# Weight copies of the next projection behind heads 1 and 2, and six recurrence tiles split during the last keys' projection

## What is computed

```python
h = rms_norm(x, attn_norm[l])
z = h @ w_in[l]
q_lat, kv_lat, k_rope_raw, g_mla, u_lru, g_lru, m_mla, m_lru = jnp.split(z, IN_SPLITS, axis=-1)
y_mla = mla_branch(q_lat, kv_lat, k_rope_raw, g_mla, cos, sin, ...)
y_lru = rglru_branch(u_lru, g_lru, conv_w[l], conv_b[l], ...)   # (h * silu(gate)) @ w_o_lru
merged = jax.nn.sigmoid(m_mla) * y_mla + jax.nn.sigmoid(m_lru) * y_lru
x = x + merged @ w_out[l]
ple_gate = jax.nn.sigmoid(rms_norm(x, ple_norm[l]) @ w_ple_gate[l])
x = x + (p[l] @ w_ple[l]) * ple_gate
```

```python
q = (rms_norm(q_lat, q_a_norm) @ w_q_b)      # per head 128 plain and 64 rotary columns
kv = (rms_norm(kv_lat, kv_a_norm) @ w_kv_b)  # per head 128 key and 128 value columns
s = (q_nope . k_nope + q_rope . k_rope) * scale
pr = softmax(where(mask, s, -inf)); o = pr @ v
return (o * silu(gate)) @ w_o
```

## Time and profile before

| | |
|---|---|
| runs (us) | 2049.51, 2050.53, 2049.27; median 2049.51 |
| profiled execution | 2050.18 us, span 2048.4 us, mean granted TensorE clock 0.991 |
| TensorE busy | 1998.9 us, 98% of the span |
| VectorE busy | 677.3 us, 33% |
| ScalarE busy | 715.6 us, 35% |
| GpSimd busy | 898.1 us, 44% |
| DMA | 247.20 MB, mean 121 GB/s |

### The profile page before, as it was taken

The page is one execution under the profiler, slowest core; times in us unless marked ns, Lnnn a source line. Parts: engine busy times, 40 slices in busy tenths (PEclk is TensorE's granted clock), DMA queues, the critical chain, the costliest instruction groups (busy, mean ns, idle before and its releaser), DMA issues.

```text
span 2048.4 us, 24912 instructions
## 1 busy us (share of the span) xinstructions
PE 1998.9 (98%) x9070; PEld 1663.5 (81%) x9070; DVE 677.3 (33%) x943; ACT 715.6 (35%) x1240; POOL 898.1 (44%) x683
## 2 busy tenths in 40 slices
PE   7999999999999999999999999899999999999996
PEld 6888888888888888888888877778888888888885
DVE  4100000000454638354555544681010250111344
ACT  6322223222253444433344544322222222333333
POOL 3444444444454545454451223154444454444552
PEclk9999999999999999999999999999999999999998
DMA  6433333333233323332462332254333343234232
GB/s 253 170 123 108 117 123 119 128 123 124 82 99 107 114 91 107 104 134 82 114 161 66 124 103 81 84 205 144 104 122 123 112 185 113 83 103 186 102 103 103
DMA packets 128697, 247.20 MB, mean 121 GB/s; under 512 B 15053, under 2 KB 40309, under 8 KB 120565
## 3 DMA queue, kind: packets, MB, share of 16 engines
q1 hardware_dynamic: 116688, 185.09, 27.9%
q10 hardware_dynamic: 11941, 61.17, 7.9%
HBM read 214.26 MB, written 29.36 MB: 119 GB/s over the span
## 4 chain that ended last, share of the span: by engine, by line
issue 60%; POOL 38%; POOLq 1%; DVE 1%; PE 0%; ACT 0%; DVEq 0%
POOL wlo L362 38%; POOLq L361 1%; POOLq L358 0%; DVE x L1270 0%; PE ps L1281 0%; DVE x L1243 0%; DVE stage L1242 0%; DVE x L1273 0%; POOLq L362 0%; ACT stage L811 0%; DVEq L126 0%; DVE nrm L848 0%; DVE nrm L853 0%; DVE nrm L854 0%; DVE nrm L847 0%
## 5 line engine op out<-in xcount | busy, mean ns | idle before, releaser
L362 POOL TENSOR_TENSOR wlo<-raw,whi 128x512 fp32r<-128x512 f32 x672 | 896.8, 1338 | 1124.7 <-ACT whi L378 1123.7
L378 ACT ACTIVATE whi<-raw 128x512 fp32r<-128x512 f32 x672 | 421.8, 631 | 1159.6 <-PE ps L1281 1109.7
L1281 PE MATMUL ps<-hhi,whi 128*128 128x512 f32 x1408 | 548.2, 389 | 1.1 <-POOL wlo L362 1.1
L1281 PE MATMUL ps<-hhi,wlo 128*128 128x512 f32 x1408 | 547.8, 389 | 0.0
L1281 PE MATMUL ps<-hlo,whi 128*128 128x512 f32 x1408 | 547.7, 389 | 0.0
L1281 PEld LDWEIGHTS ps<-hhi,whi 128*128 128x128 f32 x1408 | 264.3, 188 | 56.5 <-POOL wlo L362 1.5
L1281 PEld LDWEIGHTS ps<-hlo,whi 128*128 128x128 f32 x1408 | 264.4, 188 | 55.1 <-issue 0.2
L1281 PEld LDWEIGHTS ps<-hhi,wlo 128*128 128x128 f32 x1408 | 264.4, 188 | 54.7
L933 DVE TENSOR_TENSOR stage<-ps,stage 128x512 f32<-128x512 f32 x16 | 11.0, 691 | 412.4 <-ACT stage L475 410.9
L1281 PE MATMUL ps<-lhi,whi 128*128 128x512 f32 x256 | 101.2, 395 | 6.0 <-POOL wlo L362 3.8
L1281 PE MATMUL ps<-llo,whi 128*128 128x512 f32 x256 | 100.8, 394 | 0.0
(11 more groups left out here) (254 smaller groups left out, 2438.8 us busy)
## 6 DMA issues: line engine op xcount, KB each, us to landing
raw<-in_w_in SPq DMA_DIRECT2D x88, 1024.0 KB, 5.0
raw<-in_w_o_lru SPq DMA_DIRECT2D x16, 1024.0 KB, 5.0
raw<-in_w_o_mla SPq DMA_DIRECT2D x16, 1024.0 KB, 5.0
raw<-in_w_out SPq DMA_DIRECT2D x16, 1024.0 KB, 5.0
raw<-in_w_ple_gate SPq DMA_DIRECT2D x16, 1024.0 KB, 4.9
sig_scr<-stage ACTq DMA_DIRECT2D x8, 1024.0 KB, 7.0
raw<-in_w_kv_b SPq DMA_DIRECT2D x32, 256.0 KB, 3.9
stage<-sig_scr ACTq DMA_DIRECT2D x8, 1024.0 KB, 4.8
```

The costliest lines, as they stand in the source:

```text
L362: pool.tensor_tensor(wlo[:, k % RING], raw[:, k // RAWC, k % RAWC], whi[:, k % RING].bitcast(F32), ALU.subtract).then_inc(lo_ready, 1)
L378: act.activation(whi[:, c % RING], raw[:, c // RAWC % 2, c % RAWC], ACT.Copy).then_inc(hi_ready, 1)
L1281: return pe.matmul(o, l, r, start=start, stop=stop)
```

## The change

ScalarE's four copies of the next projection's weights stood one behind head 1's exponentials, one behind head 2's and two behind head 3's. Now two stand behind head 1's and two behind head 2's. The loop variable `h` in this code is one ahead of the head whose `turned_hi` runs, and the exponentials in it are those of head `h`.

VectorE's `split_merge` of tiles 0 to 3 is taken out of the last group's heads. Tiles 0 to 5 (`AHEAD = 6`) are split at the head of the last group, ahead of the keys' `projection_lo`, so while TensorE projects that group's keys. Behind the group the tiles 6 to 15 remain.

```diff
                         exp(h, 2)
                         exp(h, 1)
                         exp(h, 0)
-                        split(c + 2 * KL + RING + h - 1)
+                    if h < 3:
+                        split(c + 2 * KL + RING + 2 * h - 2)
+                        split(c + 2 * KL + RING + 2 * h - 1)
                     if h == 3:
-                        split(c + 2 * KL + RING + 3)
                         act.wait_ge(exp_done, 16 * g + 16)
                         act.sem_inc(released[ks], 1)
...
+            AHEAD = 6
+
...
             for g in range(NG):
                 pt = 1 - g % 2
 
+                if g == NG - 1:
+                    dve.wait_ge(l_landed, 16)
+                    for t in range(AHEAD):
+                        split_merge(lhi, llo, l_split, t)
                 projection_lo(g, 1, range(4))
...
-                if g == NG - 1:
-                    dve.wait_ge(l_landed, 16)
                 for h in range(1, 5):
...
-                    if h < 3 and g == NG - 1:
-                        split_merge(lhi, llo, l_split, 2 * h - 2)
-                        split_merge(lhi, llo, l_split, 2 * h - 1)
...
-            for t in range(KL, KD):
+            for t in range(AHEAD, KD):
```

## The result

The changed kernel takes 2017.56 us (2017.3 to 2018.58, four runs) where the kernel before takes 2049.82 (2049.27 to 2050.53, four runs): a ratio of 0.9843, interval 0.9826 to 0.986, or 32.3 us less. The prediction was 2016.2 in a range of 2013.5 to 2022.0. The profiled execution took 2017.5 us with a span of 2015.7, against 2050.18 and 2048.4.

The account below looks back on a forecast made before the run. TensorE, busy 98% of the span, bounds the kernel through its idle and half-rate time. Savings of 25.8 + 4.25 + 3.9 - 0.6 = 33.3 us gave a span of 2016.9 and a median of 2016.2 us, range 2013.5 to 2022.

Parts of the forecast that it names:

- The stops and their half rate: TensorE before each next projection's third weight chunk: four stops for `wlo` and half-rate matmuls behind them vanish, saving 25.8 us.
- Rival (a): TensorE behind the stops: only idle goes, something else keeps the half rate; 2030.2 us, chance 0.08.
- Rival (c): GpSimd's third `wlo` stays late, by ring slot or raw row; only the tile parts gain, 2042.0 us, chance 0.04.
- ScalarE's cover: Before ScalarE's next exponential: 0.51 us more copying fits in 0.85 us of idle, leaving 0.34; cost nothing.
- Rival (d): ScalarE's copies delay exponentials in eight places, TensorE waits and falls to half rate; 2056.9 us, chance 0.03.
- VectorE's `pjlo`: Attention heads: if GpSimd's extra tile held it, it would end 0.8 us later, inside 1.65 us of cover.
- The tiles out of the heads: Last group's heads 1 and 2: without VectorE's split tiles, TensorE needs group three's time, saving 4.25 us.
- the stop for `llo`: Recurrence output's fifth chunk: 2.18 us stop and 1.71 us of half rate behind it vanish, saving 3.9 us.
- Tile 7: Recurrence output, next to be late: ready 2.2 us on, while TensorE wants it 5.4 us on.
- The wait for `qr`: Last group's first scores: six tiles meeting GpSimd's make `knlo` 2.2 us late, so TensorE waits about 0.6 us.
- several subtractions of 1.7 us: Sign of a wrong forecast: VectorE's six moved tiles showing several subtractions this long.
- The bound behind it: Upper bound for the `qr` wait: 1.1 us if four block, plus at most 2.9 us of half rate, 4.0.

Follow-up runs that it names:

- e6: Changed kernel with all four of ScalarE's copies behind head 1's exponentials, instead of two there and two behind head 2's: 2019.68 us.
- e1: Changed kernel with VectorE's tiles taken back into the heads, so only ScalarE's copies are moved: 2025.3 us, ratio 0.9885 to the kernel before.
- the repeat: Later comparison of the same changed kernel, nothing altered, with the kernel before: 2016.98 us against 2048.21, ratio 0.9846.
- e3: Changed kernel with four tiles split at the head of the last group in place of six: 2021.59 us.
- e2: Changed kernel with ScalarE's copies back in their old places, so only VectorE's six tiles are moved: 2041.78 us, ratio 0.9962 to the kernel before.

## Why the prediction was right

**The stops and their half rate (25.8 us): right.** With the copies alone, the first three group distances shrink by 18.86 us, from 196.70 to 177.84 (first scores at 1088.65 and 1266.49), where 6.76 + 6.23 + 5.91 = 18.90 were predicted. The way from the stop to the transposes is 3.22 us at clock 1.00. Rival (a), that something else holds the clock down, is out: the half rate went with the stops. Rival (c) is out by GpSimd's rows.

**ScalarE's cover (nothing): right, and thin.** 0.31 us of idle is left, and `e6` lost 0.4 us per group with the exponential 0.61 us late. Rival (d) needed 2.5 us per place; 0.61 us late is more than the 0.51 that it feared of a copy, and it halved no clock. VectorE's `pjlo`, which the prediction had only bounded, was not held by GpSimd's extra tile: in the changed kernel it ran beside GpSimd's pair of 1110.22 to 1112.80 and took 1.78 us, where the earlier trace rows has 1.77.

```profile
1112.07 1.78 DVE L1124 TENSOR_TENSOR pjlo<-ps,pjhi 128x256 fp32r<-128x256 f32 x3 [0.60 <-ACT pjhi L699]
```

**The tiles out of the heads (4.25) and the stop for `llo` (3.9): right.** The second row of the ledger is 13.35 against 13.31, the third 1.65 against 1.71. Tile 7, the next in line, was not late.

**The wait for `qr` (-0.6): right in kind, 0.2 too large.** VectorE in the last group, from the first tile to `knlo` (the six tiles' casts and subtractions, then the projection's low tiles), with two of GpSimd's rows of the same time:

```profile
1250.79 0.43 DVE L1092 CAST lhi<-llo 128x512 fp32r<-128x512 f32 x1
1251.25 1.66 DVE L843 TENSOR_TENSOR llo<-llo,lhi 128x512 fp32r<-128x512 f32 x1
...
1253.28 0.69 DVE L843 TENSOR_TENSOR llo<-llo,lhi 128x512 fp32r<-128x512 f32 x1
1253.89 1.51 DVE L1092 CAST lhi<-llo 128x512 fp32r<-128x512 f32 x1
...
1256.51 1.66 DVE L843 TENSOR_TENSOR llo<-llo,lhi 128x512 fp32r<-128x512 f32 x1
...
1259.15 1.51 DVE L1092 CAST lhi<-llo 128x512 fp32r<-128x512 f32 x1
...
1261.31 2.48 DVE L1083 SCALAR_TENSOR_TENSOR knlo<-ps,knhi 128x512 fp32r<-128x512 f32 x4
...
1250.87 1.49 POOL L362 TENSOR_TENSOR wlo<-raw,whi 128x512 fp32r<-128x512 f32 x1 [3.41 <-ACT whi L378]
...
1253.54 1.59 POOL L362 TENSOR_TENSOR wlo<-raw,whi 128x512 fp32r<-128x512 f32 x1 [1.18 <-ACT whi L378]
```

Four of the twelve instructions meet a GpSimd tile and take 1.66 or 1.51 us, one for each of the four GpSimd tiles, as predicted: two are subtractions, and two are casts, a form that the prediction had not named as one that can be blocked. The six tiles take 10.5 us (1250.79 to 1261.31) instead of 6.4; the prediction's working, 1268.70 to 1279.7, had 11.0. The last group distance is 59.66 against 59.28 with five tiles, 0.4 us. One of the prediction's own signs of being wrong, several subtractions of 1.7 us, did appear, with two of 1.66. It was badly chosen, because the sum had already counted four blocked instructions. The Trainium skill has both forms ("SBUF — State Buffer", section "Who interferes with whom"): a `tensor_tensor` with both inputs in SBUF, and a cast that runs in a mode that takes the shared port pair, shut out a GpSimd instruction that reads SBUF and are shut out by it, and the one that comes second waits for the whole of the other. The rows agree for VectorE, 1.66 against 0.69 and 1.51 against 0.42.

**The bound behind it was mis-sized, to no effect.** The prediction allowed 2.9 us of half rate on top of a wait of 1.1, and argued from stops "of 2 us and more". The chip takes a wait of 2.08 us there without it. In `e1` a wait of 2.17 us for `prob` did bring it, so the length alone doesn't give the bound (the last section comes back to this). The high end of the range, 2022.0, was wider than it needed to be for that reason.

**What is left of the difference.** 2017.56 was measured against 2016.2. By the ledger 0.2 us was gained more than predicted in the stage (33.47 against 33.3), and 0.80 lost in the one profiled execution before the stage, which the repeat does not show. The medians of the changed kernel are 2017.56 and 2016.98, those of the kernel before 2049.51, 2049.82, 2049.7 and 2048.21 in different comparisons. As gains that is 32.3 us and 31.2 in the repeat against 33.3 predicted, and 33.3 lies inside both intervals (28.7 to 35.7 and 28.9 to 34.4 us). The miss of 1.0 to 2.1 us is of the size of the scatter ahead of the stage, and I give it no cause.

## What to carry to other kernels

When a producer that has been idle for microseconds causes a short stop on the bounding engine, look at the place in the order of the instruction that feeds it, before its duration: here the same work done earlier gave 6.4 us per group, of which more than a third was half-rate matmuls behind the stop. Measure the way from the stop to a landmark behind it, not the idle alone, and take the whole of it, since half rate is not a fixed surcharge. Before work is put into an engine's idle time, count how much of it will meet instructions of another engine that hold it up: six tiles took 10.5 us instead of 6.4, and one tile fewer would have been free.

## What the runs showed of the hardware that I had not expected

**Half rate does not follow from the length of a stop alone.** In one place of one program, the first score of group four, 1.15 and 2.08 us left the clock at 1.00, 3.01 us halved it, but 1.2 us after the end of the wait, and 3.93 halved it almost at once. In front of the fifth chunk a stop of 2.18 us was followed by half rate at once in the kernel before, 0.7 us later in `e3`, and not at all in `e1`. What TensorE did just before doesn't tell the three apart: its rows are the same, start for start to within 0.05 us, for 13.5 us ahead of the stop in all three, and for 19.7 us in `e1` and `e3`. What decides is open. With six and eight casts the clock fell at nearly the same time of the program, whichever wait had just ended.

**Its cost varies by two.** Behind a stop of 3.8 to 3.9 us in front of the third chunk, the way to the transposes took 5.90, 5.37, 5.06 and 6.14 us in the kernel before and 4.77 in `e2`, against 3.22 at full rate: 1.55 to 2.92 us on top of the stop. It goes with how much of the low-clock stretch lies behind the stop: all of the 6.14 us in one of them, 3.10 us in `e2`.

**A late input can cost without being listed.** In `e6` each group lost 0.4 us and the view of waits shows no row for it. It was found only by the distances of starts.
